# Opening of a two-layer encoder on one core: raw memory, gains in rows of 128, a first slab in quarters, a later tap transform, later constants, and a scatter over 64 rows

## The chip, the cores and the metric

The kernel runs on 1 core of one Trainium2 chip. The metric is device microseconds of that core, lower is better. Time before: 1711.65 us, the median of 3 runs (1711.46 to 1714.24).

## The reference, cut to what matters

All tensors are float32. `x` and `mem` are 256 rows of 1024, and there are two layers:

```python
for i in range(2):
    u = rmsnorm(h, norm_mix_g[i])
    proj = u @ w_in[i]                        # 1024 -> 7168: a, g, q, k, v, two gates
    y_conv = conformer_conv(proj[..., :2048], ...)      # a * sigmoid(g), depthwise 31 taps, norm, silu
    y_attn = diff_attention(q, k, v, positions, ...)    # rope on q and k, 8 heads of two halves
    h = h + (gate_c * y_conv + gate_a * y_attn) @ w_out[i]
    m = rmsnorm(mem, norm_mem_g[i])
    h = h + cross_attention(rmsnorm(h, norm_x_g[i]), m, w_xq[i], w_xkv[i], w_xo[i])
    h = h + hier_moe(rmsnorm(h, norm_ffn_g[i]), ...)    # 32 experts, two per token
return rmsnorm(h, final_norm_g)
```

In `cross_attention` the keys and values are `m @ w_xkv`; no order of the memory's rows matters there, since they are summed over after a softmax. `rmsnorm(mem)` is a factor for each memory row, times a gain for each column.

## The kernel before

The program is written engine by engine, with semaphores by hand; each engine runs its own list in order. A layer has two stages.

**The dense stage** works on 28 slabs of 1024 x 512 weights (2 MB each, `SLABS`), landed by SyncE into two slots. Each slab is used in four quarters. ScalarE copies a quarter into a rounded high part (`split_to`, L833), VectorE subtracts to get the low part (`low_to`, L1228), and TensorE multiplies high by high, high by low and low by high. A quarter of a slab that is used by rows (`row_jobs`) is 8 matmuls of 128x512 with the high part (L1842, L1843, in the last quarter L1811, L1812) and 4 with the low part (L1848, L1817); by columns (`columns`) it is 16 and 8 of 128x256 (L1786, L1787, L1791). Four quarters can be split ahead. SyncE issues slab n when the low parts of slab n-2 are done (`w_lo`). Results go to eight PSUM banks; `banks_of_jobs` deals the banks to jobs in the order of `JOBS`, and a job waits until its bank has been emptied.

The stage opens with the memory's keys (`xk.0`, `xk.1` from slab `xk0`), then the turned norm of h (`nm`, transposes at L1733, evacuated with the gain by ScalarE at L891 and by VectorE at L1273), the transform of the convolution's taps (`wf`, four matmuls of 31 rows at L1874, evacuated by ScalarE at L936), then the slabs a0, g0, a1, g1, and so on. In the first layer the memory comes before all that: ScalarE sums its squares (L795), VectorE builds two diagonal matrices of the inverse roots (L1157), TensorE multiplies memory by them (L1741), which norms and turns it at once, VectorE copies it to `memT` (L1167), and high and low parts are made from that copy (L910, L1293). In the first layer VectorE also computes the rope angles (L1174 to L1189) from positions and constants, and ScalarE takes their sines (L802, L803) before it goes on with splits. GpSimd issues the small parameter loads: taps after slab 0, positions, lambdas and router weights after slab 1.

**The expert stage** runs 16 pairs of experts. For each pair TensorE gathers tokens, does the up products (L2200, four of 32 output rows side by side), turns them, does the down products (L2229) and scatters (`scatter`, L2241) into the PSUM banks 4 to 7, where h stays. SyncE streams 12 MB of weights for a pair as slots come free (`freed`). After the last pair ScalarE squares what stands in the banks, for the next layer's norm (L919) or for the final norm (L1141).

## Time and profile before

| | us |
|---|---|
| median of 3 runs | 1711.65 |
| the profiled execution | 1714.48 |
| its span, first to last instruction | 1712.5 |
| mean granted TensorE clock | 0.932 |

The profiled execution's own time is 2.0 us above its span and 2.8 us above the median. The slices of the page show each layer as a dense stage (about 10 slices of 42.8 us, TensorE at 9 tenths) and an expert stage (the DMA engines at 9 tenths). A time in a row is in us from the first instruction.

### The profile page before, as it was taken

To read this page: it belongs to the slowest core of one execution; us is meant where nothing else is said; L and a number is where in the kernel's file an instruction comes from. 1 tells how busy PE (TensorE), PEld (TensorE's weight loads), DVE (VectorE), ACT (ScalarE), POOL (GpSimd) and SP (SyncE) were. 2 spreads that over 40 slices of the span, in tenths; PEclk is the share of its full clock that TensorE was granted. 3 is DMA by queue.
4 is the path that set the end of the run, shared out by engine and by line. 5 is a ranking of instruction groups with operands and counts; after the bars stand their busy time and mean duration, and the time that the engine had idled before them with its cause. 6 is when DMAs were issued, how large, how long until landed. Compare 5 with 4: busy or idle time off the path is not lost.

```text
span 1712.5 us, 23508 instructions
## 1 busy us (share of the span) xinstructions
PE 1467.7 (86%) x9702; PEld 982.6 (57%) x9702; DVE 611.5 (36%) x1017; ACT 521.2 (30%) x825; POOL 52.2 (3%) x102
## 2 busy tenths in 40 slices
PE   8999999999986867676799999999999676767776
PEld 7788889897432323232277988998864232322322
DVE  5566777654110100001064668775531000010101
ACT  6536555553100000000163465635431000000001
POOL 3011000000000000000000200000000000000000
PEclk9999999999997988888899999999999888888979
DMA  8546335667999999999954462357589999999997
GB/s 240 196 126 218 112 136 193 253 242 289 416 428 427 428 428 429 429 429 428 417 208 173 130 209 100 132 210 278 216 345 429 427 427 428 429 429 428 429 427 290
DMA packets 93279, 531.26 MB, mean 310 GB/s; under 512 B 6118, under 2 KB 6310, under 8 KB 66310
## 3 DMA queue, kind: packets, MB, share of 16 engines
q1 hardware_dynamic: 89888, 524.06, 76.2%
q0 software_dynamic: 3296, 5.98, 1.7%
q8 instruction: 60, 0.98, 0.2%
q14 instruction: 23, 0.19, 0.0%
q10 hardware_dynamic: 12, 0.05, 0.0%
HBM read 524.82 MB, written 1.05 MB: 307 GB/s over the span
## 4 chain that ended last, share of the span: by engine, by line
PE 65%; DMA 28%; DVE 3%; ACT 2%; issue 1%; PEldq 0%; DVEq 0%; SPq 0%; ACTq 0%
DMA ring<-in_w_dram 28%; PE ps L2200 16%; PE ps L1786 7%; PE ps L1791 7%; PE ps L1787 7%; PE ps L1842 4%; PE ps L1843 4%; PE ps L1848 4%; PE ps L2229 2%; PE ps L2241 2%; PE ps L2162 2%; PE ps L1817 1%; PE ps L1811 1%; PE ps L1812 1%; PE ps L1945 1%
## 5 line engine op out<-in xcount | busy, mean ns | idle before, releaser
L2200 PE MATMUL ps<-ring,work 128*32 128x512 f32 x1440 | 280.9, 715 | 192.0 <-DMA ring<-in_w_dram 184.7
L1228 DVE TENSOR_TENSOR weight_split<-ring,weight_split 128x1024 fp32r<-128x1024 f32 x224 | 270.2, 1222 | 156.8 <-ACT weight_split L833 154.4
L833 ACT ACTIVATE weight_split<-ring 128x1024 fp32r<-128x1024 f32 x224 | 234.1, 1058 | 205.6 <-PE ps L1848 76.5
L2200 PEld LDWEIGHTS ps<-ring,work 128*32 128x32 f32 x1440 | 69.1, 129 | 389.7 <-DMA ring<-in_w_dram 204.6
L1620 DVE TENSOR_TENSOR work<-tail,ps 128x256 f32<-128x256 f32 x32 | 13.5, 421 | 647.8 <-ACT tail L1120 647.8
L1786 PE MATMUL ps<-operand_split,weight_split 128*128 128x256 f32 x896 | 227.1, 291 | 1.3 <-DVE operand_split L1293 0.7
L1787 PE MATMUL ps<-operand_split,weight_split 128*128 128x256 f32 x896 | 219.8, 283 | 0.0
L2200 PE MATMUL ps<-big,work 128*32 128x512 f32 x576 | 193.5, 704 | 1.0 <-DVE work L1645 1.0
L1786 PEld LDWEIGHTS ps<-operand_split,weight_split 128*128 128x128 f32 x896 | 171.3, 191 | 16.8 <-issue 15.2
L1787 PEld LDWEIGHTS ps<-operand_split,weight_split 128*128 128x128 f32 x896 | 171.7, 192 | 1.3 <-issue 1.2
L1116 ACT ACTIVATE tail<-ps 128x512 f32<-128x512 f32 x32 | 33.8, 1055 | 430.2 <-PE ps L2200 430.2
L2162 PEld LDWEIGHTS ps<-work,big 128*128 128x128 f32 x1024 | 119.4, 192 | 37.7 <-issue 36.6
L2162 PE MATMUL ps<-work,big 128*128 128x64 f32 x1024 | 124.3, 275 | 9.6 <-PE ps L2200 9.6
L1791 PE MATMUL ps<-operand_split,weight_split 128*128 128x256 f32 x896 | 125.8, 283 | 0.6 <-DVE weight_split L1228 0.6
L2241 PE MATMUL ps<-sqo,tail 128*128 128x512 f32 x256 | 118.4, 605 | 3.3 <-DVE sqo L1624 1.6
L1791 PEld LDWEIGHTS ps<-operand_split,weight_split 128*128 128x128 f32 x896 | 115.6, 192 | 0.8 <-DVE weight_split L1228 0.8
L1842 PE MATMUL ps<-weight_split,operand_split 128*128 128x512 f32 x288 | 113.0, 393 | 1.7 <-issue 1.7
L1843 PE MATMUL ps<-weight_split,operand_split 128*128 128x512 f32 x288 | 112.2, 389 | 0.0
L1101 ACT ACTIVATE tail<-ps,cst 128x256 f32<-128x256 f32 x32 | 15.1, 473 | 312.1 <-PE ps L2241 286.0
L2229 PE MATMUL ps<-ring,work 128*32 128x512 f32 x544 | 81.7, 602 | 0.0
L2241 PEld LDWEIGHTS ps<-sqo,tail 128*128 128x128 f32 x256 | 46.0, 189 | 58.2 <-issue 45.9
L1848 PE MATMUL ps<-weight_split,operand_split 128*128 128x512 f32 x288 | 77.0, 389 | 0.0
(259 smaller groups left out, 1668.7 us busy)
## 6 DMA issues: line engine op xcount, KB each, us to landing
ring<-in_w_dram SPq DMA_DIRECT2D x118, 2048.0 KB, 28.1
big<-in_w_dram SPq DMA_DIRECT2D x56, 2048.0 KB, 27.1
ring<-in_w_in_dram SPq DMA_DIRECT2D x28, 2048.0 KB, 8.1
big<-in_w_dram SPq DMA_DIRECT2D x20, 1024.0 KB, 16.8
ring<-in_w_xkv_dram SPq DMA_DIRECT2D x8, 2048.0 KB, 8.0
ring<-in_w_dram SPq DMA_DIRECT2D x12, 1024.0 KB, 21.3
ring<-in_w_attn_out_dram SPq DMA_DIRECT2D x4, 2048.0 KB, 7.9
ring<-in_w_conv_out_dram SPq DMA_DIRECT2D x4, 2048.0 KB, 8.5
```

What stands on the lines that cost most here:

```text
L833: act.activation(split_quarter(k, 0), landed_quarter(k), ACT.Copy).then_inc(w_hi, 1)
L1228: dve.tensor_tensor(split_quarter(k, 1), landed_quarter(k), split_quarter(k, 0).bitcast(F32), ALU.subtract).then_inc(w_lo, 1)
L1786: pe.matmul(dst, hi[:, k, :], xs[0][:, k, :], start=(k == 0), stop=False)
L1787: pe.matmul(dst, hi[:, k, :], xs[1][:, k, :], start=False, stop=False)
L1791: last = pe.matmul(dst, lo[:, k, :], xs[0][:, k, :], start=False, stop=(k == DC - 1))
L1842: pe.matmul(dst[s], xh, hi[:, k, :], start=(c == 0 and k == 0), stop=False)
L1843: pe.matmul(dst[s], xl, hi[:, k, :], start=False, stop=False)
L1848: last = pe.matmul(dst[s], xs[0][:, 2 * c + k, s * P:(s + 1) * P], lo[:, k, :], start=False, stop=False)
L2162: last = pe.matmul(ps[:, 0, c * 2 * CAP:(c + 1) * 2 * CAP], uN[:, s, c * P:(c + 1) * P], sel[:, s].rearrange("p e s -> p (e s)"), start=(s ...
L2200: last = pe.matmul(ps[CAP * j:CAP * (j + 1), 1, :], xe[:, k, e * CAP:(e + 1) * CAP], up_slot(slots[j])[:, k, :], start=(k == 0), stop=(k = ...
L2229: last = pe.matmul(ps[CAP * j:CAP * (j + 1), 3, :], up_t[:, f, e, :], down_slot(slots[4 + e])[:, f, half * SLAB:(half + 1) * SLAB], start= ...
L2241: last = pe.matmul(ps[:, 4 + 2 * s + half, :], scat[:, half, s * P:(s + 1) * P], y_sb, start=False, stop=True, skip_group_check=True)
```

## The change

It does eight things:

- **Memory raw.** The diagonal matmuls go. TensorE transposes the raw memory (now with row p x 2 + s on partition p, one stretch of 8 KB), and ScalarE and VectorE make high and low parts straight from PSUM with the gain alone. The factor of each memory row is applied later: on the keys, VectorE multiplies by `mem_scale` as it empties the bank (`keys`, which takes over from ScalarE's `out`); on the values, ScalarE multiplies the turned probabilities (`xturn`, two instructions instead of one). `mem_root`, `mem_scales` and `spread_mem_scales` compute the factors, in the first layer, behind the turned norm and the rope angles.
- **Gains.** The six norm vectors come as 96 rows of 128 and are turned by one transpose instead of 16.
- **Slab 0** is landed by four DMAs with a semaphore each.
- **Values first.** The slabs `xk0` and `xv0` change places, in both layers. The keys of `xk0` are now made late, in the place of `xv0`.
- **Taps' transform.** TensorE does it behind a1 instead of ahead of a0, and ScalarE empties it ahead of g.2.
- **Order of splits.** The splits are dealt between the four parts of the turned norm, up to the first quarter of g0 (in the first layer), and ScalarE's squares of the memory and the sines stand behind them.
- **Constants.** All but the identity are issued after slab 2 instead of after slab 1.
- **Scatter.** The rows of the down product stand by half instead of by expert, so each of the four matmuls contracts 64 rows (0 to 63 or 64 to 127) instead of 128 of which half are zero, and ScalarE makes one copy of the columns instead of two masked ones. VectorE's last pair of a layer moves behind its reading of the pass count.

```diff
-SLABS = ["xk0", "a0", "g0", "a1", ... "xv0", "xv1", ...]
+SLABS = ["xv0", "a0", "g0", "a1", ... "xk0", "xv1", ...]
...
+        elif job == "g.3":
+            banks = (WHERE_TAPS,)
...
-            sp.dma_start(memN, mem[0].rearrange("(s p) d -> p s d", p=P)).then_inc(mem_in, 16)
+            sp.dma_start(memN, mem[0].rearrange("(p s) d -> p s d", p=P)).then_inc(mem_in, 16)
...
+                    if n == 0:
+                        for q in range(QUARTERS):
+                            cs = slice(2 * q, 2 * q + 2)
+                            sp.dma_start(slot(0)[:, cs, :], slab_source(name, L)[:, cs, :]).then_inc(first_slab_in[q], 16)
...
-                    if L == 0 and n == 1:
+                    if L == 0 and n == 2:
                         sp.dma_start(cst[:, P:NCON], consts[:, P:NCON]).then_inc(cst_in, 16)
...
+                    for j in range(4):
+                        act.wait_ge(st_mt, j + 1)
+                        for c in range(2):
+                            act.activation(mem_s[0][:, 2 * j + c, :], ps[:, MEM_BANKS[j], c * T:(c + 1) * T], ACT.Copy,
+                                           scale=mem_gain(L, 2 * j + c)).then_inc(mem_hi, 1)
+                        split_to(j + 1)
...
+                early_values(0)
+                if L == 0:
+                    split_to(SPLITS + 1)
                 act.wait_ge(*due(cur_ready, 1))
-                turned_high("nm", u_s, R_MIX)
                 for j in range(4):
-                    ahead(f"wf{j}")
+                    turned_high("nm", u_s, R_MIX, (j,))
+                    split_to(SPLITS + 2 + j)
+                    if j == 0:
+                        early_values(1)
                 if L == 0:
+                    mem_root()
                     angles()
...
+                for c in range(DC):
+                    turned_low("nm", u_s, R_MIX, 0, (c,))
+                    if c % 2:
+                        low_to(SPLITS + 2 + c // 2)
                 if L == 0:
                     rope_angles()
+                    mem_scales()
...
-                taps_transform()
                 row_jobs("a.", "a0", (0, 1), u_s, have=(lo_ready, 0, 2))
                 row_jobs("g.", "g0", (0, 1), u_s)
                 row_jobs("a.", "a1", (2, 3), u_s)
+                if L == 0:
+                    pe.wait_ge(cst_in, 16)
+                taps_transform()
                 row_jobs("g.", "g1", (2, 3), u_s)
+                if L == 0:
+                    pe.wait_ge(st_norm, N_DIAGONALS)
+                    for s in range(TT):
+                        last = pe.matmul(ps[:, MEM_NORM_BANK, s * P:(s + 1) * P], cst[:, C_MEAN:C_MEAN + P], mem_diag[:, s, :],
+                                         start=True, stop=True)
...
-                            last = pe.matmul(ps[:, 4 + 2 * s + half, :], scat[:, half, s * P:(s + 1) * P], y_sb,
+                            at = slice(2 * CAP * half, 2 * CAP * (half + 1))
+                            last = pe.matmul(ps[:, 4 + 2 * s + half, :], scat[at, s * P:(s + 1) * P], y_sb[at, :],
                                              start=False, stop=True, skip_group_check=True)
```

ScalarE in the opening of the first layer, from the end of the turned norm to the first splits of g0 and beyond (`operand_split<-ps,cur` is the turned norm, `big<-ps 120x512` the taps' transform, `h_u<-ps` the keys' evacuation). Before:

```order
L818 ACTIVATE h_u<-ps 128x512
L891 ACTIVATE operand_split<-ps,cur 128x256 x8
L936 ACTIVATE big<-ps 120x512 x4
L802 ACT_TABLE_LOAD
L802 ACTIVATE rope_cs<-work 128x256
L803 ACTIVATE rope_cs<-work,cst 128x256
L833 ACTIVATE weight_split<-ring 128x1024 x8
L818 ACT_TABLE_LOAD
L818 ACTIVATE work<-ps 128x512 x2
```

And now, from the last part of the turned norm on:

```order
L912 ACTIVATE operand_split<-ps,cur 128x256 x2
L854 ACTIVATE weight_split<-ring 128x1024
L812 ACTIVATE big,small<-big 128x1024 x2
L815 ACTIVATE small<-small 128x2
L820 ACT_TABLE_LOAD
L820 ACTIVATE rope_cs<-work 128x256
L821 ACTIVATE rope_cs<-work,cst 128x256
L854 ACTIVATE weight_split<-ring 128x1024 x6
L836 ACT_TABLE_LOAD
L836 ACTIVATE work<-ps 128x512 x2
```

The taps' evacuation is gone from here, the memory's squares and root stand ahead of the sines, and nine quarters are split ahead of the sines instead of seven.

TensorE around the taps' transform of the first layer (four matmuls of 120x512). Before it stood between the turned norm and a0:

```order
L1791 MATMUL ps<-operand_split,weight_split 128x256 x8
L1733 MATMUL ps<-cst,big 128x128 x16
L1874 MATMUL ps<-big,cst 120x512 x4
L1842 MATMUL ps<-weight_split,operand_split 128x512
L1843 MATMUL ps<-weight_split,operand_split 128x512
```

Now it stands between the last quarter of a1 and the first of g1:

```order
L1876 MATMUL ps<-weight_split,operand_split 128x512
L1881 MATMUL ps<-weight_split,operand_split 128x512 x2
L1939 MATMUL ps<-big,cst 120x512 x4
L1906 MATMUL ps<-weight_split,operand_split 128x512
L1907 MATMUL ps<-weight_split,operand_split 128x512
```

Three slabs now stand ahead of it. VectorE in the first instructions of the program (`memT<-ps` is the kept memory, `weight_split` a low part). Before:

```order
L1161 COPY pk<-ps 128x48 x2
L1167 COPY memT<-ps 128x512 x2
L1293 SCALAR_TENSOR_TENSOR operand_split<-memT,pk,operand_split 128x256 x2
L1167 COPY memT<-ps 128x512
L1293 SCALAR_TENSOR_TENSOR operand_split<-memT,pk,operand_split 128x256 x2
L1167 COPY memT<-ps 128x512
L1293 SCALAR_TENSOR_TENSOR operand_split<-memT,pk,operand_split 128x256 x4
L1228 TENSOR_TENSOR weight_split<-ring,weight_split 128x1024
```

Now:

```order
L1194 COPY pk<-ps 128x6x8 x2
L1348 SCALAR_TENSOR_TENSOR operand_split<-ps,pk,operand_split 128x256 x2
L1275 TENSOR_TENSOR weight_split<-ring,weight_split 128x1024
L1348 SCALAR_TENSOR_TENSOR operand_split<-ps,pk,operand_split 128x256 x2
L1275 TENSOR_TENSOR weight_split<-ring,weight_split 128x1024
L1348 SCALAR_TENSOR_TENSOR operand_split<-ps,pk,operand_split 128x256 x2
L1275 TENSOR_TENSOR weight_split<-ring,weight_split 128x1024
L1200 COPY memT<-ps 128x512
L1348 SCALAR_TENSOR_TENSOR operand_split<-ps,pk,operand_split 128x256 x2
L1275 TENSOR_TENSOR weight_split<-ring,weight_split 128x1024
```

One copy instead of four stands ahead of the last low part of slab 0, and the low parts of memory and weights alternate.

## Rows read from the trace of the kernel before

**Rows 1.** The page: TensorE and its clock in 40 slices, then the chain that ended last.

```profile
PE   8999999999986867676799999999999676767776
PEclk9999999999997988888899999999999888888979
PE 65%; DMA 28%; DVE 3%; ACT 2%; issue 1%; PEldq 0%; DVEq 0%; SPq 0%; ACTq 0%
```

**Rows 2.** Busy time by stretch: PE, PEld, DVE, ACT, POOL; clock, DMA share, GB/s.

```profile
46.00:80.00 34.00, 34.00 (x151) 28.14 (x150) 19.62 (x20) 16.47 (x17) 0.00 (x0) 1.00 0.70 247
80.00:140.00 60.00, 60.00 (x395) 48.05 (x395) 35.83 (x55) 23.17 (x29) 12.29 (x24) 1.00 0.42 132
472.00:835.00 363.00, 262.20 (x1781) 111.88 (x1778) 31.77 (x75) 28.76 (x50) 0.00 (x0) 0.85 1.01 428
```

**Rows 3.** Timeline, TensorE in the opening: start, duration, instruction, idle before, releaser.

```profile
10.82 5.47 PE L1741 MATMUL ps<-work,big 128*128 128x128 f32 x32 [1.61 <-DVE work L1157]
...
30.91 1.94 PE L1733 MATMUL ps<-cst,big 128*128 128x128 f32 x16 [0.42 <-PE ps L1791]
```

**Rows 4.** Chain that ended last, around a0's and g0's ends: start, duration, what.

```profile
43.95 1.24 DVE weight_split L1228
45.23 0.73 PE ps L1817 x2
...
57.77 0.45 PE ps L1817 x2
```

**Rows 5.** Timeline, ScalarE in the opening.

```profile
31.64 3.02 ACT L891 ACTIVATE operand_split<-ps,cur 128x256 fp32r<-128x256 f32 x8 [0.51 <-PE ps L1733]
...
37.57 1.28 ACT L802 ACT_TABLE_LOAD   x1
42.15 0.42 ACT L802 ACTIVATE rope_cs<-work 128x256 f32<-128x256 f32 x1 [3.30 <-DVE work L1189]
...
42.88 3.89 ACT L833 ACTIVATE weight_split<-ring 128x1024 fp32r<-128x1024 f32 x4
```

**Rows 6.** Timeline, VectorE in the opening: two low parts, rope angles' first and last.

```profile
27.86 2.36 DVE L1228 TENSOR_TENSOR weight_split<-ring,weight_split 128x1024 fp32r<-128x1024 f32 x2 [0.43 <-ACT weight_split L833]
...
36.68 0.29 DVE L1174 CAST rank_sums<-cst 128x256 fp32r<-128x256 f32 x1 [0.22 <-DVE operand_split L1273]
...
41.69 0.43 DVE L1189 TENSOR_SCALAR work<-work 128x512 f32<-128x512 f32 x1
```

**Rows 7.** DMA issues of line 685, slab 2 alone (issued at 25.66).

```profile
DMA to landing us min/median/max: 15.6/15.6/15.6
```

**Rows 8.** DMA issue of line 689, the constants (issued at 5.36).

```profile
DMA to landing us min/median/max: 18.7/18.7/18.7
```

**Rows 9.** Timeline, VectorE in the second layer's opening: low parts of the norm.

```profile
877.45 1.90 DVE L1273 SCALAR_TENSOR_TENSOR operand_split<-ps,cur,operand_split 128x256 fp32r<-128x256 f32 x4 [0.99 <-ACT operand_split L891]
```

**Rows 10.** Timeline, TensorE in the second layer's opening: taps, first product of a0.

```profile
878.53 1.13 PE L1874 MATMUL ps<-big,cst 31*120 31x512 f32 x8 [0.74 <-DVEq L1283]
880.53 0.47 PE L1842 MATMUL ps<-weight_split,operand_split 128*128 128x512 f32 x1 [0.87 <-issue]
```

**Rows 11.** Timeline, TensorE: two score products of 64 rows.

```profile
190.65 0.70 PE L1945 MATMUL ps<-big 64*128 64x256 f32 x4
```

**Rows 12.** Timeline: the last scatter (four matmuls), then the final squares.

```profile
1702.83 3.70 PE L2241 MATMUL ps<-sqo,tail 128*128 128x512 f32 x8 [0.81 <-DVE sqo L1624]
...
1704.85 1.02 ACT L1141 ACTIVATE h_u<-ps 128x1024 f32<-128x1024 f32 x1 [5.64 <-PE ps L2241]
...
1706.57 1.02 ACT L1141 ACTIVATE h_u<-ps 128x1024 f32<-128x1024 f32 x1
```

**Rows 13.** Chain that ended last, before the first layer's last pair.

```profile
837.59 3.79 issue
```

**Rows 14.** Single microseconds around the same pause, columns as in Rows 2.

```profile
840.00:841.00 1.00, 0.00 (x0) 0.00 (x0) 0.00 (x0) 0.00 (x0) 0.00 (x0) 0.78 1.08 451
846.00:847.00 1.00, 1.00 (x8) 0.20 (x4) 0.00 (x0) 0.00 (x0) 0.00 (x0) 0.50 1.00 418
```

**Rows 15.** Timeline, TensorE: cross attention's last turn of probabilities, first layer.

```profile
382.52 0.66 PE L2042 MATMUL ps<-cst,work 128*128 128x128 f32 x4 [1.13 <-DVE work L1507]
```

More of the change, by code:

```diff
@@ L320, in encoder @@
         v = rows(3)
-        xv = rows(5)
         gate_c = chunks(4)
@@ L427, in encoder @@
         mixer_done = sem("mixer_buffers_free")
+        first_slab_in = [sem(f"first_slab_quarter_{q}_landed") for q in range(QUARTERS)]
         slab_in = [sem(f"dense_slab_landed_{i}") for i in range(LAND)]
@@ L883, in turned, with turned_high @@
                                 ins.then_inc(free[b], 1)
-                def turned_high(kind, dst, row):
-                    for j in range(4):
+                def turned_high(kind, dst, row, jobs=range(4)):
+                    for j in jobs:
                         b = bank(f"{kind}{j}")
@@ L1021, in _ @@
                 act.activation(ssq, ssq, ACT.Sqrt).then_inc(o_root, 1)
-                out("xk.2", xkT[:, 4:6, :], xk_ready, 3)
+                ahead("xk.2")
                 for j in range(4):
@@ L1027, in _ @@
                                    ACT.Copy, scale=sub_col).then_inc(hi_ready, 1)
-                out("xk.3", xkT[:, 6:8, :], xk_ready, 4)
+                ahead("xk.3")
                 for j, g in enumerate((gate_c, gate_a)):
@@ L1043, in _ @@
                 scale_rows(1, [1])
-                for j in range(2):
-                    out(f"xv.{j}", xv[:, j % 2, 0:SLAB], xv_ready, j + 1)
+                ahead("xk.1")
                 turned_high("nx", x_s, R_X)
                 for j in range(2, 4):
-                    out(f"xv.{j}", xv[:, j % 2, SLAB:2 * SLAB], xv_ready, j + 1)
+                    out(f"xv.{j}", xv_halves[1][:, j % 2, :], xv_ready, j + 1)
                 def xexp(hd):
@@ L1274, in low, with turned_low @@
                                              ALU.subtract).then_inc(ready, 1)
-                def turned_low(kind, dst, row, n):
-                    for c in range(DC):
+                def turned_low(kind, dst, row, n, columns=range(DC)):
+                    for c in columns:
                         low(f"{kind}{c // 2}", dst, c, 1, (hi_ready, n + 2 * (c // 2) + 2), par[:, c, row:row + 1], lo_ready)
@@ L1735, in turn_rows @@
                 return last
-            pe.wait_ge(st_mn, TT)
+            for _ in range(2):
+                pe.matmul(ps[:, 0, 0:P], ident, ident, start=True, stop=True)
+            pe.wait_ge(mem_in, 16)
             for j in range(4):
-                for c in range(2):
-                    for s in range(TT):
-                        last = pe.matmul(ps[:, 2 + j, c * T + s * P:c * T + (s + 1) * P],
-                                         memN[:, s, (2 * j + c) * P:(2 * j + c + 1) * P], mem_diag[:, s, :], start=True,
-                                         stop=True)
-                last.then_inc(st_mt, 1)
+                turn_rows(ps[:, MEM_BANKS[j], :], memN, j).then_inc(st_mt, 1)
             u = pe.alloc_register("pe_unit")
@@ L1912, in _ @@
                 row_jobs("a.", "a1", (2, 3), u_s)
+                if L == 0:
+                    pe.wait_ge(cst_in, 16)
+                taps_transform()
                 row_jobs("g.", "g1", (2, 3), u_s)
+                if L == 0:
+                    pe.wait_ge(st_norm, N_DIAGONALS)
+                    for s in range(TT):
+                        last = pe.matmul(ps[:, MEM_NORM_BANK, s * P:(s + 1) * P], cst[:, C_MEAN:C_MEAN + P], mem_diag[:, s, :],
+                                         start=True, stop=True)
+                    last.then_inc(st_norm, 1)
                 forward(0)
@@ L2228, in down_product @@
                             e, half = j // 2, j % 2
-                            last = pe.matmul(ps[CAP * j:CAP * (j + 1), 3, :], up_t[:, f, e, :],
+                            g = 2 * half + e
+                            last = pe.matmul(ps[CAP * g:CAP * (g + 1), 3, :], up_t[:, f, e, :],
                                              down_slot(slots[4 + e])[:, f, half * SLAB:(half + 1) * SLAB], start=(f == 0),
```

231 lines of the change are left out of this document (130 added, 101 removed).

## The prediction

> **What bounds the kernel now.** I read the page first: TensorE is busy at 9 tenths through each layer's dense stage, and in the expert stage at 6 to 8 with a lower clock; the chain that ended last is 65% TensorE and 28% DMA [rows 1]. The windows say why. From 46 us on the dense stage keeps TensorE busy without a gap at the full clock, 34.00 of 34 us and 60.00 of 60, while VectorE and ScalarE are at half and less. In 472 to 835 the DMA engines are at 1.01 and 428 GB/s with TensorE busy for 262 of 363 us [rows 2]. So a matmul taken out of the middle of an expert stage is worth nothing, and one that delays or advances the whole dense stage is worth its full time, since the expert loads are released by the dense stage's progress. Then the timelines of the two openings, for what TensorE waits for there, and the end.
>
> **First layer, the part before the rope angles.** The step that matters is where the first layer's TensorE becomes gapless. Before, that is at 45.23: the last quarter of a0 waits for a low part made at 43.95 [rows 4], which waits for a split at 42.88, which stands on ScalarE behind the sines at 42.15, which wait 3.30 us for VectorE's rope angles, begun at 36.68 [rows 5, 6]. The question is when these angles begin in the changed kernel; call it R.
>
> The memory's norm leaves the path: before, its diagonal product starts at 10.82 and takes 5.47 us, part of it at half clock [rows 3]; now the transposes need only memory and gains, and I take their start at 9.2. ScalarE then needs for each of four rounds two copies of 0.38 (3.02 / 8) and a split of 0.97 (3.89 / 4), 1.75 in all [rows 5]; VectorE needs two of 0.48 (1.90 / 4) [rows 9] and a low part of 1.18 (2.36 / 2) [rows 6], 2.1. VectorE is the slower. From about 10.7, four rounds and one kept copy of some 0.7 end at 20.0. There slab 2 is issued, 5.7 us before the 25.66 of now [rows 7]. TensorE's values end at 22.5 to 24; the turned norm of h, its transposes 1.94 in all [rows 3], starts there. Its four rounds on VectorE, each again 2.1 us and each with a low part between, run from about 25 to 33.5, and the first low part of g0 follows: 34.7. **R is 34.8**, if slab 2 and the constants have landed by then.
>
> **First layer, from the angles on.** The angles take 5.4 us (36.68 to 42.12) [rows 6]. New behind them are the memory's variance and root, two instructions on two columns, at most 0.4 (the last step of the angles, on 512 columns, takes 0.43 [rows 6]). Then comes the table load of 1.28, no longer hidden in the wait as it was at 37.57, the two sines (0.73 from 42.15 to 42.88) and one split of 0.97 [rows 5]. With 0.3 of hand-overs that makes R + 9.1 = 43.9 for the second quarter of g0. Only g0's first quarter has been split ahead of the sines, and TensorE has finished it by about 40. So the wait on the angles is not gone; it moves from a0's last quarter to g0's second, one and a quarter slabs later in TensorE's list. A quarter is 2.72 us (45.96 to 58.22 are four and a half [rows 4]); three of them end g0 at R + 17.3 = 52.1, against 58.22 now. From this comes a loss: TensorE stands still for about 4 us. After a stop of 3.79 us the granted clock was 0.50 and still so 5 us after the restart [rows 13, 14], which would cost half of that, 2.7; between nothing and 3 I take 2.0. **g0 ends at 54.1, a gain of 4.1.**
>
> The taps' transform is now inside the gapless part and costs its 1.13 us [rows 10]. The bank of g.3 waits for ScalarE to empty the first of the four: 0.3, at most the 0.87 that TensorE waited behind the same instructions before [rows 10]. The memory factors' two small matmuls before the forward transform cost 0.45 (a quarter of the 1.94 for 16 transposes, if one costs two of those; between 0.24 and 0.9). Left of the first opening: 4.1 - 1.1 - 0.3 - 0.5 = **2.2 us**.
>
> **Second layer.** Before, a0 starts at 880.53: the norm's low parts are there from 878.4 (877.45 and two of 0.48 [rows 9]), and then come the taps, 1.13, and 0.87 of wait for a bank that ScalarE empties behind them [rows 10]. Now a0 needs only the first two low parts. The scatter's 1.8 us (below) and VectorE's earlier end of the pair help little, because VectorE's list (eight memory parts, low parts, the sum of h) sets the pace of the first slab: the slab's end moves by 0.9. That puts a0 at 877.2, 3.3 earlier; less 1.1 for the taps and 0.3 for the bank, **1.9 us**.
>
> **Scatter.** Four matmuls take 3.70 us, 0.93 each [rows 12]. With 64 rows, two can lie side by side. The trace has two neighbours of that: four matmuls of 31 rows and 512 columns in 1.13 us together, hardly more than one [rows 10], and two score products of 64 rows in 0.70 [rows 11], where a lone one of 256 columns would be half of 0.93 and two in turn 0.93. I take 1.9 for the four. The Trainium skill says the same (TensorE: Matmul & The Clock Gate, Part 3: Packing small matmuls): tiles in different row groups run together, four row tiles of 512 columns at 3.07 times one after the other; the trace's 1.13 against 3.70 makes 3.3. In all pairs but the last of a layer the DMA hides the gain, since the loads are the later ones [rows 2]. At the very end, the two halves of h are squared one after the other by ScalarE, starting at 1704.85 and 1706.57 [rows 12]: the first starts 0.9 earlier, the second is then held by the first one's chain, **0.9 us**.
>
> **At nothing:** gains as 96 rows (hidden behind memory's landing; it may save some tenths); one copy of scatter columns for two (TensorE's turn of the up product waits for other things); the split copy in cross attention, 0.38 instead of part of a copy, four times a layer, because TensorE's wait in that place is for VectorE's scaling [rows 15], at most 0.2 each and 1.6 in all; the key factors on VectorE, which was half idle, 35.83 of 60 [rows 2].
>
> **Sum.** 2.2 + 1.9 + 0.9 = 5.0 us. The profiled execution of 1714.48 (span 1712.5) would come to 1709.5; from the median, 1711.65, to **1706.7 us**. 0.2% is 3.4 us, about what a measurement of this kernel can tell from no change, so "faster" begins below 1708.2.
>
> **Rivals.**
> 1. *No clock loss, and an earlier R.* If the clock holds and R is 33.7, g0 ends at 51.0: 3.1 us more, total 8.1, 1703.6. For it: nothing in the list forbids it. Against: the stop of 3.79 us [rows 13].
> 2. *Slab 2 and the constants arrive late.* Slab 2 took 15.6 us because the small loads of GpSimd ran beside it [rows 7]; these are now released about 2 us earlier, too. Issued at 20.0 it would land at 35.6, and the constants, 0.7 MB issued behind it, at 38 to 39. With R = 39.2, g0 ends at 58.1 with 1.6 of clock loss: gain 0.1, less 1.9, plus 2.8 elsewhere: 1.0 in all, 1710.7. From R = 40.2 on, all is lost.
> 3. *Slower.* The same place, one step more: the constants take their 18.7 us from issue [rows 8] and the 2 MB of slab 3, issued at about 31, share the engines with them (5 us at 428 GB/s [rows 2]). R = 20.4 + 18.7 + 5 = 44; the total is then 3.8 us slower, 1715.5. What speaks against it: the 18.7 were spent behind 4 MB of others.
> 4. *The clock in the first products.* In the opening the matmuls with diagonals become transposes, and the clock was 0.50 there before during part of the 5.47 us [rows 3]. If the values start at half clock, they end 3 us later, R becomes 36.9, g0 ends at 55.8: total 3.3, 1708.4. The Trainium skill has the rule for it (same page, Part 4: PE-mode transpose): a transpose does not count as work for the clock. No row here separates the two; the 16 transposes at 30.91 are too short.
> 5. *The scatter does not pair.* Then 0.9 and 0.3 are missing: 3.8, 1707.9.
>
> **How the numbers follow.** Chances: forecast 0.46 (its own range 1705.0 to 1708.6), rival 1 0.18, rival 2 0.14, rival 3 0.05, rival 4 0.11, rival 5 0.06. Range 1702.8 to 1711.0: it holds rivals 1, 2, 4 and 5 and leaves out rival 3 and the tails. Faster: 0.42 of the forecast, rival 1, half of rivals 4 and 5, 0.68. Slower 0.05. The rest, 0.27, the same.
>
> **What would show it.** In the profile after: four low parts of slab 0 done near 20; slab 2 landed by 33 and the first rope instruction near 35; TensorE idle about 4 us after g0's first quarter, with the clock at 0.50 behind it; g0's end near 54; a0 of the second layer near 3 us earlier against the end of the pair's products; the scatter at 1.9 us. If the angles start after 39, or if TensorE never stands there, the forecast is wrong in that step, and the sum with it.

## The result and the profile after

The changed kernel takes 1719.22 us, the median of 6 runs (1715.92 to 1720.71), against 1711.66 (1710.39 to 1714.24) for the kernel before on the same chip. The ratio is 1.0035, with a 95% interval of 1.0025 to 1.0046: slower, where 5 us less were forecast, above the stated range (to 1711.0) and above rival 3 (1715.5). The profiled execution took 1720.71 us, its span 1718.9, its mean granted clock 0.926 (before: 1714.48, 1712.5, 0.932). The medians and ratios below leave out two executions, one of e5 (2057.98 us) and one of e8 (1773.01 us), whose mean granted clock was 0.641 and 0.806.

The page of the changed kernel, TensorE and its clock in 40 slices and the chain that ended last, answers [rows 1]:

```profile
PE   8999999999966757575799999999998575757575
PEclk9999999999987988888899999999999797988888
PE 62%; DMA 31%; DVE 3%; ACT 2%; issue 2%; ACTq 0%; PEldq 0%; DVEq 0%; SPq 0%
```

TensorE's busy digits are lower through the expert stages, as the scatter there is shorter. The chain has 2% of "issue" where it had 1%: time in which the chain stands and the profile shows nothing waited for. It is not spread over the kernel. Here is the chain from the last scatter but one of the first layer to the end of the last pair's up products (start, duration, what), which answers [rows 13]:

```profile
834.53 1.99 PE ps L2316 x8
836.51 5.61 issue
842.12 4.47 PE ps L2273 x17
846.59 0.96 issue
847.54 7.30 PE ps L2273 x47
```

And the same place in the second layer:

```profile
1680.87 1.99 PE ps L2316 x8
1682.85 5.36 issue
1688.22 1.91 PE ps L2273 x3
1690.13 3.52 issue
1693.64 9.21 PE ps L2273 x61
```

The scatter takes 1.99 us, as forecast. But the pause behind it grew from 3.79 to 5.61, so the restart is no earlier; and inside the up products there is a second stop, which the kernel before has nowhere. It comes after 17 of the 64 matmul records in one layer and after 3 in the other. The weights' halves meet at record 32, so it is no wait for data. The clock is at half meanwhile. Windows around the second layer's stop, with the columns of [rows 2]:

```profile
1687.00:1688.00 1.00, 0.00 (x0) 0.00 (x0) 0.00 (x0) 0.00 (x0) 0.00 (x0) 0.85 0.99 418
1690.00:1693.00 3.00, 0.13 (x1) 0.00 (x0) 0.00 (x0) 0.00 (x0) 0.00 (x0) 0.50 1.02 418
1696.00:1697.00 1.00, 1.00 (x8) 0.19 (x4) 0.00 (x0) 0.00 (x0) 0.00 (x0) 0.50 1.05 434
1698.00:1699.00 1.00, 1.00 (x16) 0.29 (x11) 0.00 (x0) 0.00 (x0) 0.00 (x0) 1.00 1.04 434
```

At 0.50 TensorE gets 8 records done in a microsecond, at 1.00 it gets 16.

Of the DMA queues two are marked "instruction"; the one called q8 has the larger packets (16,384 bytes each in the trace), and they are few. The page gives it (queue, kind: packets, MB, share of 16 engines):

```profile
q1 hardware_dynamic: 89856, 524.05, 75.9%
...
q8 instruction: 62, 1.02, 0.2%
```

That is 16.4 KB a packet. Asked by stretch for the first layer's end, 839 to 841, 841 to 845 and 845 to 847 us:

```profile
q1 hardware_dynamic: 106, 0.79, 96.2%
q8 instruction: 1, 0.02, 3.4%
...
q1 hardware_dynamic: 235, 1.70, 102.2%
...
q1 hardware_dynamic: 109, 0.80, 97.3%
q8 instruction: 1, 0.02, 3.4%
```

In the trace the first packet starts at 839.38 and takes 1.10, and TensorE restarts at 842.12, 1.64 behind its end; the second starts at 845.09, takes 1.09, and TensorE's second stop ends at 847.54. In the second layer the packets start at 1685.48 and 1691.33, and the stops end at 1688.22 and 1693.64. Between 580 and 830 us, while TensorE runs its loop over the pairs, there is no such packet. The kernel before has them too, at 838.62 and 844.40 with the restart at 841.37, and at 1683.93 and 1689.75 with the restart at 1686.69, but no second stop.

Where the rest of the time went, from the timelines of TensorE (us; one profiled execution each):

| | before | after |
|---|---|---|
| first matmul of the forward transform, layer 1 | 79.82 | 79.78 |
| first token gather, layer 1 | 420.21 | 420.94 |
| from the 15th to the 16th scatter of layer 1 | 26.46 | 29.24 |
| from there to the forward transform of layer 2 | 63.79 | 63.51 |
| from there to the gather of layer 2 | 340.75 | 341.14 |
| from the 15th to the 16th scatter of layer 2 | 23.32 | 29.22 |

The two last pairs lost 2.8 and 5.9 us. In the profiles of this case that have no second stop, this stretch takes 23.3 to 26.5 us, so 29.2 is beyond what varies from one execution to the next, but how much each stop cost is known to 3 us only. The openings, which were to give 4 us, gave nothing.

### The profile page after: what moved, and what is told of

The parts are those of the page before. It is cut to its first block, busy times and chain, and to the rows that moved or that the text cites. A ratio compares the mean times of both kernels' runs of the same rounds, so it can differ in the third digit from the quotient of the medians.

```text
span 1718.9 us, 23441 instructions
## 1 busy us (share of the span) xinstructions
PE 1416.5 (82%) x9673; PEld 957.9 (56%) x9673; DVE 616.5 (36%) x1026; ACT 503.5 (29%) x793; POOL 52.3 (3%) x102
## 4 chain that ended last, share of the span: by engine, by line
PE 62%; DMA 31%; DVE 3%; ACT 2%; issue 2%; ACTq 0%; PEldq 0%; DVEq 0%; SPq 0%
DMA ring<-in_w_dram 31%; PE ps L2273 16%; PE ps L1850 7%; PE ps L1855 7%; PE ps L1851 7%; PE ps L1906 4%; PE ps L1907 4%; PE ps L1912 3%; PE ps L2303 1%; PE ps L2235 1%; PE ps L1875 1%; PE ps L1881 1%; PE ps L1876 1%; PE ps L2018 1%; PE ps L1950 1%
## 5 line engine op out<-in xcount | busy, mean ns | idle before, releaser
L2273 PE MATMUL ps<-ring,work 128*32 128x512 f32 x1440 | 285.6, 719 | 242.2 <-DMA ring<-in_w_dram 230.3
L2273 PE MATMUL ps<-big,work 128*32 128x512 f32 x576 | 194.8, 710 | 4.5 <-issue 3.5
L1906 PE MATMUL ps<-weight_split,operand_split 128*128 128x512 f32 x288 | 114.7, 398 | 6.1 <-ACT weight_split L854 3.1
L1144 ACT ACTIVATE tail<-ps 128x256 f32<-128x256 f32 x32 | 12.3, 383 | 260.8 <-PE ps L2316 235.1
L2303 PE MATMUL ps<-ring,work 128*32 128x512 f32 x544 | 81.7, 602 | 0.0
L2303 PE MATMUL ps<-big,work 128*32 128x512 f32 x480 | 74.4, 603 | 2.0 <-DVE work L1694 2.0
L2316 PE MATMUL ps<-sqo,tail 64*128 64x512 f32 x256 | 63.6, 615 | 3.3 <-DVE sqo L1698 1.6
```

The lines of the kernel that those rows point to most:

```text
L1906: pe.matmul(dst[s], xh, hi[:, k, :], start=(c == 0 and k == 0), stop=False)
L2273: last = pe.matmul(ps[CAP * j:CAP * (j + 1), 1, :], xe[:, k, e * CAP:(e + 1) * CAP], up_slot(slots[j])[:, k, :], start=(k == 0), stop=(k = ...
L2303: last = pe.matmul(ps[CAP * g:CAP * (g + 1), 3, :], up_t[:, f, e, :], down_slot(slots[4 + e])[:, f, half * SLAB:(half + 1) * SLAB], start= ...
L2316: last = pe.matmul(ps[:, 4 + 2 * s + half, :], scat[at, s * P:(s + 1) * P], y_sb[at, :], start=False, stop=True, skip_group_check=True)
```

## The experiments

**Theory F (instruction loading).** TensorE's instructions come in packets. Behind its loop a branch jumps over the code for further passes, about 1180 instructions that are never executed here, so the code of the last pair has to be fetched; the packet that holds the jump's target is used from the target on, and the next one starts 5.7 to 5.9 us behind the first. The change took TensorE instructions out of the opening, so all later code stands elsewhere in its packets, and the target came to stand near a packet's end. The Trainium skill has this mechanism (Runtime: NRT & Kernel Launch, "Instruction fetch mechanics"): blocks of 16 KiB or 256 instructions, fetched in sequence, and a taken branch whose target isn't in the window stalls until its page is there. The size agrees with the 16.4 KB above. The page also calls the fetch mostly hidden otherwise, and the trace of the kernel before agrees: packets start at 95.3, 114.7 and 133.7 us while TensorE is busy for 60.00 of 60 [rows 2]. The window of two pages that the page names doesn't fit TensorE here: a loop of 881 instructions, more than three such blocks, ran without a packet; the page's other figure, room for 2048 instructions of TensorE, holds such a loop. A float32 matmul shows as two matmul records and two weight loads, a transpose or a rounded matmul as one of each. Each record, those of the sequencer too, counted as one instruction and the loop's body counted once, the trace has about 7270 instructions between the two stops of the changed kernel; with the 1180 that are never executed (a count from the program) that is 8451, against 33 x 256 = 8448. The rivals: **theory S**, the shorter scatter only lengthens the pause, and the clock falls for it; **theory D**, VectorE's last pair behind its reading of the pass count delays something; and the opening's changes alone.

**e1**: the changed kernel and nothing but unexecuted code.

```diff
                 with pe.If(passes > 1):
+                    for _ in range((12, 0)[L]):
+                        pe.matmul(ps[:, 0, 0:P], ident, ident, start=True, stop=True)
                     with pe.Fori(1, passes) as _p:
```

> The changed kernel, with 12 extra matmuls written into the first layer's branch for further passes, which is never taken: nothing more is executed, but the code of TensorE behind the branch stands 48 instructions later. Theory F (instruction loading): the stops of 0.96 us (first layer's last pair, after 17 records) and 3.52 us (second layer's, after 3 records) stand where a 16 KB packet of instructions ends; with the shift the first packet behind the jump holds 47 instructions more and both stops go. Stop and half clock together cost 2.7 and about 4 us, so 6 to 7 us less: 1712.5 to 1714. Theory S (the shorter scatter only lengthens the idle time, and the clock falls for it) or theory D (VectorE's last pair behind its reading of the pass count): code position plays no part, no change, 1718 to 1720, the stops stay.

Measured: 1711.74 us (1709.75 to 1715.48), ratio to before 1.0001 (0.9992 to 1.0010). Both stops are gone; the second layer's chain reads:

```profile
1675.43 4.79 issue
1680.22 9.85 PE ps L2273 x64
```

Some 6 us by the ratios, 7.5 by the medians, hung on 48 instructions that never run. Theories S and D cannot make that. (The two profiles differ by 11.2 us in span; of these, 8.4 lie in the two last pairs and 1.6 in a fall of the clock in the opening, told of below, which has nothing to do with the 48 instructions.)

**e2**: the kernel before with 50 such matmuls (range((50, 0)[L])).

> The kernel before, with 50 extra matmuls in the same branch that is never taken: TensorE's code behind it stands 200 instructions later, which by my count puts the end of an instruction packet where the changed kernel has it, some 40 instructions behind the jump in the first layer and some 10 in the second. Theory F: the same stops appear in the kernel before, about 1 us after 17 or 18 records in the first layer's last pair and 3 to 3.5 us in the second's, with the clock at half for longer: 4 to 7 us more, 1716 to 1719. Theories S and D: 1711.7, no such stops.

Measured: 1716.35 us (1714.14 to 1721.26), ratio 1.0025 (1.0015 to 1.0035). The stops appear in the kernel before, after 18 and 5 records:

```profile
840.57 5.32 PE ps L2200 x18
845.89 0.33 issue
846.22 5.38 PE ps L2200 x46
...
1683.06 1.92 PE ps L2200 x5
1684.98 3.35 issue
1688.34 9.26 PE ps L2200 x59
```

The first is shorter than expected, and the total lies at the low end of what was expected. The first layer's last pair, at 26.0 us, shows no loss that can be told from chance; the second's, at 29.1, does.

**e9**: as e1 with 4 matmuls in place of 12, a dose between.

> The changed kernel with 4 unexecuted matmuls (16 instructions) in the first layer's branch in place of the 12 of e1: a dose between. By theory F the end of the first packet moves back against TensorE's code by 16 instructions of 4 a matmul, that is 8 records: in the first layer's last pair the stop then stands after 9 records instead of 17, and is longer, near 3 us, since the second packet comes 5.8 us behind the first whatever TensorE has used up; in the second layer the packet's end falls behind the whole last pair, no stop. Total near 1714 to 1716, between the changed kernel and e1. If the stops have another cause than packets: no stop after 9 records.

Measured: in the first layer the stop stands exactly after 9 records and takes 2.77 us; the second layer has none:

```profile
841.32 2.76 PE ps L2273 x9
844.09 2.77 issue
846.86 7.94 PE ps L2273 x55
...
1682.93 5.44 issue
1688.37 9.96 PE ps L2273 x64
```

The time missed: 1718.59 us (1717.52 to 1719.93), ratio 1.0046 (1.0032 to 1.0061), not 1714 to 1716. From the 15th to the 16th scatter of the first layer it took 29.8 us against 24.2 to 26.5 in all profiles without a stop there: 3.3 to 5.6 for a stop of 2.8, with the half clock behind it, where the expectation had allowed 2 to 4 for everything. The profiles themselves add up: against e1's, e9's span is 8.3 us longer, 5.6 of it in this last pair, 0.4 in the second one and 1.6 in the opening's fall of the clock; against the changed kernel's it is 2.9 shorter, 3.0 of it in the second last pair. Why the medians don't show these 3 us (1718.59 against 1719.22, and the ratios the other way about), four runs don't settle. So the places of the stops are shown, their price is not.

**e3**: the kernel before with the scatter alone.

```diff
-                    act.activation(scat[:, 0, :], ps[:, 2, 0:T], ACT.Copy, scale=cst[:, C_MLO:C_MLO + 1])
-                    act.activation(scat[:, 1, :], ps[:, 2, 0:T], ACT.Copy,
-                                   scale=cst[:, C_MHI:C_MHI + 1]).then_inc(scat_ready, 1)
+                    act.activation(scat, ps[:, 2, 0:T], ACT.Copy).then_inc(scat_ready, 1)
...
+                            at = slice(2 * CAP * half, 2 * CAP * (half + 1))
-                            last = pe.matmul(ps[:, 4 + 2 * s + half, :], scat[:, half, s * P:(s + 1) * P], y_sb,
+                            last = pe.matmul(ps[:, 4 + 2 * s + half, :], scat[at, s * P:(s + 1) * P], y_sb[at, :],
```

> The kernel before with the scatter by 64 rows alone (one copy of the columns, rows of the down product by half, four matmuls over 64 rows); TensorE's instructions are as many as before, so the packets end where they did. Theory F: no second stop; scatter 1.9 instead of 3.70; TensorE's restart ahead of the last pair doesn't move, since it waits for its instructions from a fixed time behind the scatter's start (idle 5.6 instead of 3.8), so of the gain only the last scatter's 0.9 us is left, less about 1 us for a longer half clock in each layer: 1710.5 to 1712.5. Theory S: the longer idle is what cost the changed kernel its 2.7 and 4 us: 1716 to 1718. The prediction's own view: 0.9 from the end and 0.9 of the second opening, 1710.

Measured: 1712.44 us, ratio 0.9997 (0.9988 to 1.0006), the pause ahead of the last pair 5.65 and 5.30. The first packet starts 4.9 and 4.5 us behind the scatter's start, as before (4.7 and 4.4), and TensorE restarts 1.7 behind its end: the restart hangs on the packet, not on the scatter. In the second opening a0 starts 20.5 us behind the scatter's start, before 20.2: nothing of the shorter scatter arrives there. As theory F had it.

**e4**: the changed kernel with the old scatter, padded as e1.

> The changed kernel without its scatter (over 128 rows with two masked copies, as before), with the same 12 matmuls in the branch never taken, so that no packet of instructions ends in the last pairs. Theory F: no second stop; what is left is the opening's changes, which the traces put at nothing in the first layer's opening and about +1.5 us in the rest (the taps' transform +0.7, slab by columns +0.6 in each layer), less 1 in the second opening: 1711.5 to 1713.5. Theory D: VectorE's order is still the changed one: 1716 or more. The prediction's own view, opening alone: 1707.6.

Measured: 1713.03 us, ratio 0.9999 (0.9990 to 1.0008). The opening alone is worth nothing that these runs can tell (their interval is 1.5 us to either side), and theory D is out.

Now the opening's missing gain. Two of its terms could be tried, each on e1, and a third thing at the end (e6).

**e5**: the taps' transform between a0 and g0, where TensorE stands anyway.

```diff
+                if L == 0:
+                    pe.wait_ge(cst_in, 16)
+                taps_transform()
                 row_jobs("g.", "g0", (0, 1), u_s)
                 row_jobs("a.", "a1", (2, 3), u_s)
-                if L == 0:
-                    pe.wait_ge(cst_in, 16)
-                taps_transform()
```

> The changed kernel with the 12 unexecuted matmuls (as e1), and the taps' transform moved from behind a1 to between a0 and g0, emptied by ScalarE ahead of the memory's root (g.1, a.2, a.3 and g.2 take its banks). If the prediction's term for the transform (1.13 + 0.3 a layer) is what was too small (the traces show 1.06 of work, 0.76 of wait, and restarts and a wait ahead of the forward transform, some 2.7 in the second layer): in the first layer the transform now lies in the stop of 3 us on the angles; g0's second quarter starts up to 0.9 later, since ScalarE empties four banks first, and 2.7 are saved behind a1: 1.8 less. In the second layer 2.0 stand ahead of g0 in place of 2.7: 0.7 less. In all 2 to 2.5 us below e1. If the transform is not what ate the gain: within 1 us of e1.

Measured: 1712.59 us, ratio 1.0005 (0.9995 to 1.0015). A miss. g0's second quarter came at 47.32, 1.9 later than in e1: ScalarE emptied four banks ahead of the memory's root and the sines. And g.2 and all later jobs had got other banks, with a new wait of 0.80 us at 139.12. e10 takes both away.

**e6**: the second layer's last pair ahead of the branch, so that no jump stands before it.

> The changed kernel with the 12 unexecuted matmuls (as e1), and in the second layer TensorE's last pair written ahead of the branch for further passes instead of behind it (the further passes then end with their own), so that it follows the loop without a jump. Theory F (instruction loading): the idle time of 5.2 us ahead of the last pair is gone, up products start within 1 us of the scatter's end; then they wait for their second halves, which in e1 landed at 1683.7, against 1690.0 for the end of the products; the second down halves landed at 1694.6 with the down product ending near 1698.2. So 1 to 1.5 us less than e1, no more, because the weights become the bound. If the idle time is not the jump but the reading of the pass count or the data: same as e1.

Measured: 1712.51 us, ratio 1.0002 (0.9992 to 1.0011). The mechanism was right, the gain wasn't there. Timeline of TensorE: the up products start 0.44 us behind the scatter and stand again at their second half, now for weights:

```profile
1677.78 0.62 PE L2273 MATMUL ps<-ring,work 128*32 128x512 f32 x1 [0.44 <-DMA ring<-in_w_dram]
1687.69 1.06 PE L2273 MATMUL ps<-ring,work 128*32 128x512 f32 x1 [6.27 <-DMA ring<-in_w_dram]
```

The last weights bound the end at nearly the same time, and the jump, now behind the last pair, adds: from the last scatter's start to the end of the span it is 10.2 us, in e1 8.8.

**e7**: TensorE's 16 transposes of the memory ahead of the gains' transpose.

```diff
-            pe.wait_ge(par_in, 16 * 6)
-            pe.transpose(ps[:, ROW_BANK, 0:GAINS], big[0:GAINS, 0, 0:P], ident[0:GAINS, 0:GAINS]).then_inc(st_rows, 1)
...
             for j in range(4):
                 turn_rows(ps[:, MEM_BANKS[j], :], memN, j).then_inc(st_mt, 1)
+            pe.wait_ge(par_in, 16 * 6)
+            pe.transpose(ps[:, ROW_BANK, 0:GAINS], big[0:GAINS, 0, 0:P], ident[0:GAINS, 0:GAINS]).then_inc(st_rows, 1)
```

> The changed kernel with the 12 unexecuted matmuls (as e1), and TensorE's 16 transposes of the memory placed ahead of the gains' transpose, so that they don't wait for the six gain loads (landed at 9.8). The transposes start at about 7 instead of 11.0, ScalarE's first copy at about 11 instead of 12.1, and since VectorE's list is full from there to the angles, the angles start about 1 us earlier than 36.6, and so does g0's second quarter: 0.5 to 1 us less than e1. If slab 2 and the constants set the angles instead, nothing: same as e1.

Measured: 1709.98 us (1706.37 to 1712.00), ratio 0.9987 (0.9977 to 0.9997). The transposes start at 6.94 and not at 10.99 as in the changed kernel, the rope angles at 35.88 and not at 36.60, g0's second quarter at 44.76 and not at 45.47. That is 0.7 us, and the ratio is 2.4 us below e1's: the intervals of the two overlap, so more than the 0.7 is not shown.

**e8**: e5, e6 and e7 together.

> The last three together, on the changed kernel with the 12 unexecuted matmuls. If the three terms are independent: 3.5 to 5 us below e1, 1707 to 1708, and so faster than the kernel before by 0.2 to 0.3%. If DMA transfers take over as the bound after a shorter opening: 1 to 2 us below e1 only.

Measured: 1712.63 us, ratio 1.0005 (0.9994 to 1.0016). What e7 gives is gone again. e5's new waits, which are in this kernel too, and e6's later jump are the likely takers; the run doesn't part them.

**e10**: e7 and the transform between a0 and g0, with two differences to e5: only g.1, a.2 and a.3 change banks (to 1, 3 and 4, which the transform's parts leave), and ScalarE empties only the first part ahead of the root.

```diff
+                if L == 0:
+                    mem_squares()
+                taps_out(0)
+                if L == 0:
+                    mem_root()
+                    angles()
+                for j in range(1, 4):
+                    split_to(SPLITS + 5 + j)
+                    taps_out(j)
```

> As e7 (memory's transposes ahead of the gains'), and the taps' transform between a0 and g0 as in e5, but with the PSUM banks of g.2 and of all later jobs as in the changed kernel, and only the first of its four parts emptied by ScalarE ahead of the memory's root, the others between the splits behind the sines. In e5 the sines came 1.9 us later than in e1 and TensorE waited 0.8 for a bank at 139, which both ate the gain. If these two were the cause of e5's miss: 1 to 2 us less than e7 (1709.98), g0's second quarter within 0.8 of e7's 44.76 and no wait near 139: 1708 to 1709. If the place of the transform is worth nothing anyway: same as e7.

Measured: **1707.97 us** (1704.76 to 1709.83), ratio 0.9978 (0.9969 to 0.9987), 0.2% faster than the kernel before. TensorE has the transform and two short stops where it had one of 2.79 us, and the clock stays at 1.00 from 40 to 56 us:

```profile
38.12 1.14 PE L1943 MATMUL ps<-big,cst 31*120 31x512 f32 x8
40.01 0.47 PE L1910 MATMUL ps<-weight_split,operand_split 128*128 128x512 f32 x1 [0.76 <-issue]
43.71 0.50 PE L1910 MATMUL ps<-weight_split,operand_split 128*128 128x512 f32 x1 [0.71 <-ACT weight_split L855]
```

The forward transform starts at 74.33, in e7 at 77.50, before at 79.82. Not all of the 3.2 us against e7 is the transform's place: in e7's profile the clock was at 0.50 from 13 to 16 us, among the first products, and in e10's it was not, so the turned norm's transposes start at 24.36 there and at 25.41 in e7. That part is an accident of the execution.

**e11** is e7 with the old scatter, **e12** is e10 with the old scatter.

> As e7, but with the scatter over 128 rows as before (3.70 instead of 1.99 us). If theory S holds as a second, smaller term (the restart ahead of a last pair hangs on the instructions and not on the scatter, so the shorter scatter only adds 1.7 us of idle time and 3.4 us at half clock in a layer, about 1.7 us lost, against 0.9 us gained at the very end): 0.5 to 1.5 us less than e7, 1708.5 to 1709.5. If the scatter is worth the 0.9 to 1.8 us of the prediction: 1711 to 1712.

Measured: 1713.53 us (1709.02 to 1717.22), ratio 1.0008 (0.9997 to 1.0019).

> e10 and e11 together. If both terms are right and add up: 1707 to 1708, 0.3% below the kernel before. If the terms are nothing: 1710.

Measured: 1709.45 us (1704.84 to 1710.50), ratio 0.9983 (0.9974 to 0.9992). From e11 to e12 nothing changes but the transform's place, its banks and its emptying, both ran on the same chip, and their intervals lie apart: this, more than e10 against e7, shows that the place is worth something. Their medians differ by 4.1 us; e12's forward transform, with the clock's fall at 14 us as in e7, starts at 75.67, 1.8 ahead of e7's; the rest can be the clock's fall behind the stop that e12 no longer has, 2.8 us in e11's profile. So the old scatter is not the better one, and theory S as a second term falls: it was read from one profile each, where the half clock of a last pair varies. What the new scatter is worth stays open. By the ratios it gains 0.5 us on the kernel before (e3), loses 0.3 between e4 and e1, gains 0.9 between e12 and e10 and 3.6 between e11 and e7, and each of these is known to about 2 us only. Of the last, e11's profile shows a part that has to do with the opening: the fall of the clock told of below cost it 2.8 us behind the stop, and e7 nothing there.

The doses side by side (us, one profile each; the last pair is from the 15th to the 16th scatter; the other runs have no second stop, and 24.0 to 26.3 us for each last pair):

| | stop after records (us), layer 1; 2 | last pair 1 | last pair 2 | median |
|---|---|---|---|---|
| before | none; none | 26.5 | 23.3 | 1711.66 |
| after | 17 (0.96); 3 (3.52) | 29.2 | 29.2 | 1719.22 |
| e1 | none; none | 24.2 | 25.9 | 1711.74 |
| e2 | 18 (0.33); 5 (3.35) | 26.0 | 29.1 | 1716.35 |
| e9 | 9 (2.77); none | 29.8 | 26.2 | 1718.59 |
| e10 | none; none | 25.6 | 24.2 | 1707.97 |

## Why the prediction was wrong

**The step that failed** is a term that the prediction put at nothing without a reason: what a change costs by moving TensorE's code. It quoted "837.59 3.79 issue" [rows 13] as a stop after which the clock was low [rows 14], and used it for the price of another stop. It did not ask what ended it, and so the last pairs behind it stood in no term. "Issue" says that the profile shows nothing waited for; with TensorE's loop just over and a branch ahead, the candidates were few, and the queue marked "instruction" stood on the page. Nothing in the sum stood for code that moves against its packets, and none of the five rivals did. The runs showed in its place a second stop of 0.96 and 3.52 us inside the last pairs, which goes with 48 unexecuted instructions. That is the difference between the changed kernel's ratio of 1.0035 and e1's of 1.0001: some 6 us by the ratios, 7.5 by the medians.

The **sum itself**, freed of this by e1, still forecast 5.0 us of gain where there was none (1.0001). In the changed kernel's profile, outside the last pairs, the parts are: nothing up to the first forward transform, 0.8 us lost from there to the gather, 0.3 won in the second opening, 0.4 lost behind it, 0.9 won at the end, together nothing. The terms one by one:

- *Start of the opening.* The transposes were taken to start at 9.2. They started at 10.99, behind gains that had landed for the transpose at 9.87. "Gains as 96 rows: at nothing" was wrong by sign in this: ahead of the memory's transposes they held them up. The 16 took 3.62 us, where the same 16 in the turned norm take 1.94 at 26.12, and 1.91 in e7: the pace of half the clock. (The windows print 1.00 there; the first change of clock in this trace is one to 1.00 at 15.17.) Of the products behind them only the first two were slower, 0.78 and 0.55 instead of 0.39, so what rival 4 priced, slow products, did not come, but its slow clock did, in the transposes; whether they kept it low or the stop of 2.77 us ahead of them, these rows don't tell. Timelines of TensorE and VectorE in the changed kernel, answering [rows 3, 6]:

```profile
9.87 0.42 PE L1794 MATMUL ps<-cst,big 96*128 96x96 f32 x1 [2.77 <-DMA big<-in_norm_ffn_g_dram]
...
10.99 3.62 PE L1800 MATMUL ps<-cst,big 128*128 128x128 f32 x16
```

```profile
36.60 0.28 DVE L1221 CAST rank_sums<-cst 128x256 fp32r<-128x256 f32 x1
```

  R was 36.60, not 34.8, as late as the transposes; e7 got back 0.7 of it. Slab 2 landed at 33.8 and the constants at 36.4, 0.2 ahead of their use, so rivals 2 and 3 did not come about, the one for the constants narrowly.
- *From the angles on.* R + 9.1 was right: g0's second quarter started at 45.47, R + 8.9, after a stop of 2.79 (4 forecast). g0 ended at 55.4, 2.8 earlier than before, not 4.1.
- *The clock's fall* was forecast at 2.0, between 0 and 3. From g0's second quarter to g1's start it took 21.2 us in e1, e6 and e7, 22.8 in the changed kernel, e4 and e9, and 24.0 in e11: it costs nothing, 1.6 or 2.8, by execution. On this point the forecast and rival 1 are both right, in different runs. The changed kernel and e1 execute the same code there and differ, so it isn't the kernel that decides. Here the changed kernel's row of g0's second quarter, and the window behind it (columns as in [rows 2], 0.76 is the clock):

```profile
45.47 0.50 PE L1906 MATMUL ps<-weight_split,operand_split 128*128 128x512 f32 x1 [2.79 <-ACT weight_split L854]
```

```profile
43.00:50.00 7.00, 4.53 (x13) 3.59 (x14) 4.61 (x5) 5.33 (x7) 0.00 (x0) 0.76 0.13 47
```

- *The taps' transform* was the mis-sized term: 1.13 and 0.3 were summed. In the second layer a0 to the forward transform takes 46.28 us, before 43.61: 2.67, made of 1.1 for the work, 0.76 for the wait on the bank (the row says "issue"; ScalarE empties the transform's first bank from 915.01 to 915.60, and the product starts at 915.75), 0.40 ahead of the forward transform, and matmuls that start slower after each stop (0.47 for the first, 0.23 in the stream). Answering [rows 10]:

```profile
881.00 0.47 PE L1906 MATMUL ps<-weight_split,operand_split 128*128 128x512 f32 x1 [0.68 <-DVE operand_split L1320]
...
915.75 0.47 PE L1906 MATMUL ps<-weight_split,operand_split 128*128 128x512 f32 x1 [0.76 <-issue]
927.28 1.95 PE L1950 MATMUL ps<-big,cst 128*120 128x512 f32 x4 [0.40 <-issue]
```

  What it saved ahead of a0 there is 2.0. So the move lost 0.7 in a place without a stop, and paid only where it filled one, as e12 against e11 shows.
- *The exchanged slabs.* The late slab is now used by columns, four quarters of 2.88 us, and was used by rows, four of 2.72. The prediction left this out. From the forward transform to the gather it was 341.16 us against 340.39 in the first layer, and 0.4 more in the second. The early slab, where the gain of the same size stood against it, lies in a stretch where VectorE sets the pace; that it brought nothing there is argued, no run tries it alone.
- *Second opening.* a0 starts 17.2 us behind the last scatter's start, before 20.2: the 3.0 agree with the forecast 3.3, but the scatter has next to no part in them (e3, with the short scatter alone, 20.5; e4, without it, 17.5). With 2.67 of taps against it, 0.3 are left of the forecast 1.9.
- *Scatter.* Its 1.9 us were right (1.99), and 0.84 us at the very end too: from its start to ScalarE's square 1.18 us and not 2.02 [rows 12]. But "in all pairs but the last the DMA hides the gain" missed the last pair's own start, which the packet holds: the 1.7 us went into the pause.

## What to carry to other kernels

Where a chain shows "issue" behind a loop or a branch, look for packets of the instruction queue there: a change of the code far ahead moves the packets' ends, and a few unexecuted instructions in a branch not taken can put them back. Before a difference of some 0.3% between two kernels is believed, look at where the stops stand in both profiles, and run each at more than one padding. An operation moved into a gapless stretch costs its work, the wait for its bank and the restarts behind it (2.67 us here for 1.13 of work); moved into a stop it costs little or nothing, if it leaves the banks of others and the order of the engine that empties it as they were. When a weight stream sets the end, taking a pause away ahead of the last products only moves the wait to the next landing.

## What the hardware showed that was not expected

- Under streaming weights (410 GB/s and more in the windows around it) the packet starts 4.4 to 5.0 us behind the start of the scatter ahead of the branch, whether that scatter takes 3.70 or 1.99 us, takes 1.1 us, and TensorE restarts 1.6 to 1.7 us behind its end. The next one starts 5.6 to 6.0 us behind the first, also when TensorE has used up its instructions and stands by then, as in the changed kernel's second layer (stop from 1690.13, packet at 1691.33). This holds for both layers of all 14 profiles but the second layers of e6 and e8, where no branch stands there and the pause is 0.4 us.
- TensorE's loop over the pairs, some 880 instructions by the count above, ran without one packet between 580 and 830 us, so its code was kept; that of a target some 1200 instructions further had to be fetched.
- A stop of 2.8 us in the first opening is followed by a half clock in some executions (the changed kernel, e11) and not in others (e7): 22.8, 24.0 and 21.2 us for the same matmuls. e1's, of 3.4 us, is not.
